# Softmax attentions of a two-block transformer: values at rest in TensorE, outputs turned back by head pairs, query tiles from last to first

## The reference, cut to what matters

```
def mla_attention(q_nope, q_rope, k_nope, k_rope, v):
    ...
        s = einsum('bqhd,bkhd->bhqk', qn, k_nope) + einsum('bqhd,bkd->bhqk', qr, k_rope)
        causal = key_pos[None, :] <= qpos[:, None]
        p = softmax(where(causal, s * scale, neg), axis=-1)
        return einsum('bhqk,bkhd->bqhd', p, v)

def dsa_attention(q, k, v, q_idx, k_idx, w_idx, topk):    # one key and value head for 4 query heads
    ...
        p = softmax(where(valid, einsum('bqhd,bhqj->bhqj', qb, k_sel) * scale, neg), axis=-1)
        return einsum('bhqj,bqjd->bqhd', p, v_sel)

def native_sparse_attention(...):                          # 2 key and value heads, 3 query heads each
    ...
        o_s = einsum('bgrqn,bgqnd->bqgrd', masked_softmax(s_s, key_pos <= tq), v_sel)
        o_w = einsum('bgrqn,bngd->bqgrd', masked_softmax(s_w, m_w), vw)
        return gt[:, :, 0] * o_c + gt[:, :, 1] * o_s + gt[:, :, 2] * o_w
```

## Time and profile before

| what | value |
|---|---|
| time of three runs, median | 3297.77 us (3294.56 to 4249.05) |
| time of the profiled execution | 3300.15 us |
| its span, first to last instruction | 3298.4 us |
| mean granted TensorE clock, share of full | 0.984 |
| PE busy | 3144.2 us, 95% |
| PE weight loads (PEld, beside PE) | 2651.6 us, 80% |
| VectorE (DVE) busy | 1812.1 us, 55% |
| ScalarE (ACT) busy | 1302.5 us, 39% |
| GpSimd (POOL) busy | 391.2 us, 12% |

### The profile page before, as it was taken

The page is one execution under the profiler, slowest core; times in us unless marked ns, Lnnn a source line. Parts: engine busy times, 40 slices in busy tenths (PEclk is TensorE's granted clock), DMA queues, the critical chain, the costliest instruction groups (busy, mean ns, idle before and its releaser), DMA issues. The chain is left out here.

```text
span 3298.4 us, 48870 instructions
## 1 busy us (share of the span) xinstructions
PE 3144.2 (95%) x19216; PEld 2651.6 (80%) x19216; DVE 1812.1 (55%) x3220; ACT 1302.5 (39%) x2692; POOL 391.2 (12%) x374
## 2 busy tenths in 40 slices
PE   8999999999999999979999999999899999999996
PEld 6878788877878888868888878888788878788885
DVE  4875443425865424337566457474475565574744
ACT  4454432334354413233374333233443653332324
POOL 1031000001040000001213302010004034010100
PEclk9999999999999999989999999999999999999998
DMA  4111222212202222132100122222222000222230
GB/s 169 55 52 39 90 91 101 90 69 91 74 1 77 90 99 93 51 105 104 65 1 2 40 83 99 91 101 87 73 99 85 1 2 28 83 93 93 93 110 35
DMA packets 37342, 239.55 MB, mean 73 GB/s; under 512 B 4464, under 2 KB 5232, under 8 KB 15088
## 3 DMA queue, kind: packets, MB, share of 16 engines
q1 hardware_dynamic: 36528, 234.21, 20.1%
q10 hardware_dynamic: 576, 2.10, 0.2%
HBM read 234.19 MB, written 2.10 MB: 72 GB/s over the span
## 5 line engine op out<-in xcount | busy, mean ns | idle before, releaser
L265 PE MATMUL ps<-b_hl,bff_whl 128*128 128x512 f32 x704 | 274.1, 389 | 3.1 <-DVE b_hl L667 3.1
L267 PE MATMUL ps<-b_hl,bff_whl 128*128 128x512 f32 x704 | 273.9, 389 | 0.0
L266 PE MATMUL ps<-b_hl,bff_whl 128*128 128x512 f32 x704 | 273.9, 389 | 0.0
L248 DVE SCALAR_TENSOR_TENSOR bff_whl<-ring,b_cols,bff_whl 128x512 fp32r<-128x512 f32 (+1 forms) x224 | 153.2, 745 | 197.3 <-ACT bff_whl L235 197.1
L245 DVE TENSOR_TENSOR aff_whl<-ring,aff_whl 128x512 fp32r<-128x512 f32 x160 | 99.8, 685 | 222.8 <-ACT aff_whl L233 222.7
L235 ACT ACTIVATE bff_whl<-ring,b_cols 128x512 fp32r<-128x512 f32 (+1 forms) x224 | 136.6, 682 | 176.4 <-PE ps L267 176.4
L266 PE MATMUL ps<-aff_whl,a_u 128*128 128x512 f32 x512 | 204.3, 399 | 0.0
L265 PE MATMUL ps<-a_hl,aff_whl 128*128 128x512 f32 x512 | 199.5, 390 | 3.1 <-DVE a_hl L667 3.1
L265 PE MATMUL ps<-aff_whl,a_u 128*128 128x512 f32 x512 | 201.7, 394 | 0.0
L267 PE MATMUL ps<-aff_whl,a_u 128*128 128x512 f32 x512 | 200.7, 392 | 0.0
L267 PE MATMUL ps<-a_hl,aff_whl 128*128 128x512 f32 x512 | 199.2, 389 | 0.0
(11 more groups left out here) (524 smaller groups left out, 7746.5 us busy)
## 6 DMA issues: line engine op xcount, KB each, us to landing
ring<-in_a_w_ff SPq DMA_DIRECT2D x64, 1024.0 KB, 4.6
ring<-in_b_w_up SPq DMA_DIRECT2D x32, 1024.0 KB, 4.7
ring<-in_a_w_in SPq DMA_DIRECT2D x16, 1024.0 KB, 5.9
ring<-in_b_w_down SPq DMA_DIRECT2D x16, 1024.0 KB, 4.6
ring<-in_b_w_in_att SPq DMA_DIRECT2D x12, 1024.0 KB, 4.7
ring<-in_b_w_up SPq DMA_DIRECT2D x16, 768.0 KB, 4.0
ring<-in_b_w_in_conv SPq DMA_DIRECT2D x12, 768.0 KB, 4.2
ring<-in_a_w_out SPq DMA_DIRECT2D x8, 1024.0 KB, 4.8
```

Of the source, the lines that this page charges most:

```text
L248: self.c.nc.vector.scalar_tensor_tensor(out=self.part(j, 1, k), in0=src[:, k, :], scalar=g[:, row + k:row + k + 1], in1=self.part(j, 0, k) ...
L265: nc.tensor.matmul(bank, sh, mh, start=start, stop=False)
L266: nc.tensor.matmul(bank, sh, ml, start=False, stop=False)
L267: return nc.tensor.matmul(bank, sl, mh, start=False, stop=stop)
```

## The change

A pair of heads is now the unit of output, and three things change in `softmax_attention`:
- The query tiles of a head run from last (t = 3, 512 keys) to first (128 keys). ScalarE copies the turned probabilities into a pT that keeps all four query tiles of a head, for two heads; the widest tile of each head is copied by VectorE (semaphore lastT).
- The value product has the values at rest: at unit (h, j) key tile j meets all query tiles from j on, since those have run: one product with (4 - j) x 128 moving columns, into bank 6. The tile at rest is 128 columns wide: 64 values of the head and 64 zeros, on the left for the first head of a pair and on the right for the second, so that both heads sum into one bank, the first in rows 0 to 63, the second in rows 64 to 127. The four tiles of both heads are one sum of eight products.
- After a pair VectorE copies bank 6 to oT (semaphore lifted), PE turns oT back with four transposes into bank 7 (returned), and VectorE multiplies from there by reciprocal sums and gates for both heads at once. Bank 6 is the only one of its kind: the first value product of the next pair waits on lifted.

In mla the causal mask is added by a product as in the others, with two tiles rounded by ScalarE in the stage ahead. `place` is GpSimd's new first job in each stage: zero fills beside the values (one of 4 x 4 x 64 columns in mla, two of 4 x 64 in dsa), in nsa two copies and two fills of 4 x 64. The nsa heads are paired across the key heads (0 with 3, 1 with 4, 2 with 5), and so is the order in which their queries are split.

```diff
+    def __init__(self, scores, values, mask, out, gate=None):
+        self.scores, self.values, self.mask, self.out, self.gate = scores, values, mask, out, gate
+def softmax_attention(c, name, pairs, place, meanwhile=None, beside=None, ready=None):
...
-    units = [(h, t) for h in range(len(heads)) for t in range(TT)]
-    U = len(units)
+    units = [(h, t) for h in range(2 * len(pairs)) for t in reversed(range(TT))]
+    U, last = len(units), TT - 1
+    by_act = lambda u: sum(t < last for _, t in units[:u + 1])
+    begins = lambda u: 0 <= u < U and units[u][1] == last
+    ends_pair = lambda u: 0 <= u < U and units[u][0] % 2 == 1 and units[u][1] == 0
...
+        p, pT = sb("p", [P, 3, SEQ]), sb("pT", [P, 2, TT, SEQ])
+        negmax, rsum, weight = sb("negmax", [P, 8]), sb("rsum", [P, 2, TT, 2]), sb("weight", [P, TT, 2])
+        oT, tmp = sb("oT", [P, SEQ]), sb("o", [P, TT, 2, HD])
+        wide = weight[:].unsqueeze(3).broadcast_to([P, TT, 2, HD])
+        turned_of = lambda u: c.ps[:, 4 + u % 2, 0:(units[u][1] + 1) * P].rearrange("p (j q) -> p j q", q=P)
+        kept_of = lambda u: pT[:, units[u][0] % 2, 0:units[u][1] + 1, units[u][1] * P:(units[u][1] + 1) * P]
...
+            @block.gpsimd
+            def _(pool):
+                step = Steps(pool, pool_step)
+                place(step).then_inc(placed, 1)
+                if meanwhile is not None:
+                    meanwhile(pool, step)
             @block.tensor
             def _(pe):
-                for i in range(U + 4):
+                for i in range(U + 6):
                     if i < U:
                         h, t = units[i]
                         nk = (t + 1) * P
                         if i >= 4:
                             pe.wait_ge(probs, i - 3)
-                        if t == 0 and ready is not None:
+                        if t == last and ready is not None:
                             ready(pe, beside_done, h)
...
+                        ident, mask = pairs[h // 2].mask(t)
+                        for n, (q, k) in enumerate(pairs[h // 2].scores(h % 2, t)):
+                            nc.tensor.matmul(c.ps[:, i % 4, 0:nk], q, k, start=(n == 0), stop=False)
+                        nc.tensor.matmul(c.ps[:, i % 4, nk - mask.shape[1]:nk], ident, mask,
+                                         start=False, stop=True).then_inc(scores, 1)
                     u = i - 2
                     if 0 <= u < U:
                         pe.wait_ge(probs, u + 1)
-                        if u >= 2:
-                            pe.wait_ge(probsT, u - 1)
+                        if begins(u - 2):
+                            pe.wait_ge(lastT, units[u - 2][0] + 1)
+                        elif u >= 2:
+                            pe.wait_ge(probsT, by_act(u - 2))
                         for j in range(units[u][1] + 1):
                             ins = nc.tensor.transpose(c.ps[:, 4 + u % 2, j * P:(j + 1) * P],
                                                       p[:, u % 3, j * P:(j + 1) * P], c.ident)
                         ins.then_inc(turned, 1)
                     u = i - 4
                     if 0 <= u < U:
...
+                        h, j = units[u]
+                        if j < last:
+                            pe.wait_ge(probsT, by_act(u))
+                        else:
+                            pe.wait_ge(lastT, h + 1)
+                            if h == 0:
+                                pe.wait_ge(placed, 1)
+                            elif h % 2 == 0:
+                                pe.wait_ge(lifted, h // 2)
+                        ins = nc.tensor.matmul(c.ps[:, 6, j * P:], pairs[h // 2].values(h % 2, j),
+                                               pT[:, h % 2, j, j * P:], start=(h % 2 == 0 and j == last),
+                                               stop=(h % 2 == 1 and j == 0), skip_group_check=True)
+                        if j == 0:
+                            ins.then_inc(outs, 1)
+                    u = i - 6
+                    if ends_pair(u):
+                        n = units[u][0] // 2
+                        pe.wait_ge(lifted, n + 1)
+                        if n:
+                            pe.wait_ge(kept, n)
+                        for t in range(TT):
+                            ins = nc.tensor.transpose(c.ps[:, 7, t * P:(t + 1) * P], oT[:, t * P:(t + 1) * P], c.ident)
+                        ins.then_inc(returned, 1)
                 c.stay_busy(pe, 0, 8)
             @block.vector
             def _(dve):
                 step = Steps(dve, step_sem)
-                for i in range(U + 5):
+                for i in range(U + 7):
                     if i < U:
-                        h, t = units[i]
-                        nk, mask = (t + 1) * P, heads[h].masks(t)
+                        nk = (units[i][1] + 1) * P
                         dve.wait_ge(scores, i + 1)
...
                         nc.vector.tensor_reduce(negmax[:, i % 8:i % 8 + 1], c.ps[:, i % 4, 0:nk],
                                                 AX.X, ALU.max, negate=True).then_inc(maxed, 1)
                         if beside is not None:
                             beside(dve, beside_done, i)
+                    u = i - 2
+                    if begins(u):
+                        h = units[u][0]
+                        dve.wait_ge(turned, u + 1)
+                        if h >= 2:
+                            dve.wait_ge(outs, h - 1)
+                        nc.vector.tensor_copy(kept_of(u), turned_of(u)).then_inc(lastT, 1)
                     u = i - 5
...
+                    if ends_pair(u):
+                        n = units[u][0] // 2
+                        dve.wait_ge(outs, 2 * n + 2)
+                        if n:
+                            dve.wait_ge(returned, n)
+                        nc.vector.tensor_copy(oT[:], c.banks(6)).then_inc(lifted, 1)
+                    u = i - 6
+                    if ends_pair(u):
+                        n = units[u][0] // 2
+                        pair = pairs[n]
+                        o = c.banks(7).rearrange("p (t b d) -> p t b d", t=TT, b=2)
+                        dve.wait_ge(probs, u + 1)
+                        step(nc.vector.reciprocal(weight[:], rsum[:, n % 2]))
+                        if pair.gate is not None:
+                            step(nc.vector.tensor_tensor(weight[:], weight[:], pair.gate, ALU.mult))
+                        dve.wait_ge(returned, n + 1)
+                        if pair.gate is None:
+                            nc.vector.tensor_tensor(pair.out, o, wide, ALU.mult).then_inc(kept, 1)
                         else:
...
+                            step(nc.vector.tensor_tensor(tmp[:], o, wide, ALU.mult))
+                            nc.vector.tensor_tensor(pair.out, pair.out, tmp[:], ALU.add).then_inc(kept, 1)
             @block.scalar
             def _(act):
-                for i in range(U + 3):
+                for i in range(U + 2):
                     if i < U:
                         h, t = units[i]
                         nk = (t + 1) * P
                         act.wait_ge(maxed, i + 1)
                         if i >= 3:
                             act.wait_ge(turned, i - 2)
-                        if t == 0 and h >= 4:
-                            act.wait_ge(kept, h - 3)
+                        if t == last and h % 2 == 0 and h >= 4:
+                            act.wait_ge(kept, h // 2 - 1)
                         nc.scalar.activation(p[:, i % 3, 0:nk], c.ps[:, i % 4, 0:nk], ACT.Exp,
                                              bias=negmax[:, i % 8:i % 8 + 1],
-                                             accum_out=rsum[:, h % 4, t:t + 1]).then_inc(probs, 1)
+                                             accum_out=rsum[:, h // 2 % 2, t, h % 2:h % 2 + 1]).then_inc(probs, 1)
                     u = i - 2
-                    if 0 <= u < U:
-                        nk = (units[u][1] + 1) * P
+                    if 0 <= u < U and not begins(u):
+                        h, t = units[u]
                         act.wait_ge(turned, u + 1)
...
+                        if t == last - 1 and h >= 2:
+                            act.wait_ge(outs, h - 1)
+                        nc.scalar.copy(kept_of(u), turned_of(u)).then_inc(probsT, 1)
...
-                transpose_tiles(c, "mlaT", jobs)
+                def rounded(act):
+                    nc.scalar.copy(ident_m[:], c.ident)
+                    nc.scalar.copy(causal_m[:], c.causal)
+                transpose_tiles(c, "mlaT", jobs, None, rounded)
+                def zeros_beside_values(step):
+                    return nc.gpsimd.memset(kv4[:, :, 1::2, 0:MLA_NOPE], 0.0)
...
+                two = lambda a: a.rearrange("p t (b d) -> p t b d", b=2)
                 softmax_attention(c, "mla", [
...
+                    AttentionPair(lambda b, t, n=n: [(qT[0:MLA_QK, 2 * n + b, t * P:(t + 1) * P],
```

(45 more changed lines are left out.)

82 lines of the change are left out of this document (16 added, 66 removed).

## The result

The changed kernel takes 3345.59 us (median of three runs, 3342.49 to 3347.08) where the kernel before takes 3297.77: ratio 1.0148, 95% interval 1.0119 to 1.0178. One run of the kernel before came out slow, at 4249.05, and the ratio is taken without it. The change costs 48 us; I forecast 63. The interval leaves no doubt that it is slower, but by the limit of about 2% that is still no change, and it lies in the range.

The account below looks back on a forecast made before the run. PE was taken to bound the attention stages. Value products +20.3, turning +11.0, mask +4.5 and -1.9, new wait +27.9 and +4.3, fills and ends -1, small waits -2 gave +63.1: 3361 us, range 3328 to 3385.

Parts of the forecast that it names:

- The new wait: PE at pair starts waits for VectorE's copy of bank 6: 18 times 1.55 us, +27.9, plus 4.3 for side jobs.
- rival 4: Stalls at pairs lower the granted clock, 1.7 us lost at each of 24 pairs: +41, 3402 us; chance 0.07.
- Rival 1: The wait for the copy of bank 6 is mostly absorbed: 3333 us; chance 0.13.
- Value products: On PE, eight wide records replace twenty narrow ones a head, priced by their columns like f32 scores: +20.3 us.
- Rival 2: Wide value product records on PE are cheap, nearly as cheap as narrow ones: 3286 us; chance 0.04.
- Mask product: In mla, 64 mask products on PE at 0.07 us: +4.5; a wait gone with VectorE's add: -1.9.
- Turning back: Four PE transposes per pair of heads, 0.46 us for each of 24 pairs: +11.0 us.
- Small nsa waits: Small waits of PE in the nsa stages partly go: -2 us.
- rival 3: At transposes of nsa's 512-key unit, VectorE or ScalarE comes 0.4 us late in 24 heads: +10, 3371; chance 0.14.
- fills and ends: Filling the pipeline with the widest unit first and ending stages with the narrow one: -1 us in all six stages.
- The signs that I had named: Expected in the profile after: wide records 0.43 us apart, mla head 6.4 us, nsa head about 5.6, waits for VectorE's copy.
- The sign for "too fast": PE waiting for ScalarE at transposes in each head, or granted clock below 0.95 inside stages, would show the forecast too fast.

Follow-up runs that it names:

- narrow run: The changed kernel with each value product cut to 128 query columns, 768 of 1280 columns a head left out: 3296.72 us, ratio to before 0.9997.
- copy first: The changed kernel with VectorE's copy of bank 6 put ahead of the maximum of the same step: 3316.32 us, ratio to before 1.0059.
- two banks: The changed kernel with pairs summed in banks 6 and 7 by turns and turned back into the same bank: 3318.55 us, ratio to before 1.0068.
- both copies first: The changed kernel with VectorE's copy of bank 6 ahead of the maximum and ScalarE's copy ahead of its exponential: 3309.68 us, ratio to before 1.0036.
- the copy of ScalarE alone: The changed kernel with only ScalarE's copy of the turned probabilities ahead of the present unit's exponential: 3338.12 us, ratio to before 1.0121.
- the kernel with 64-column products: The changed kernel with each value product cut to 64 query columns, the rest left out: 3305.00 us, ratio to before 1.0019.

## Why the prediction was right or wrong

The direction, the verdict and the main cause were right; the size was 15 us too large.

*The new wait: right in mechanism and place, and nearer in size than it deserved.* I had 18 x 1.55 + 4.3 = 32.2 us. There are 18 waits, 1.41 late in a plain one; the one behind nsa's side job is 1.97 idle. Taking them away gives 27 and 29 us, but some 5 of these are lower clock (rival 4). That leaves 22 to 24 for the waits themselves, 8 to 10 under my sum: the chain was 0.14 shorter each time, and a little of the standing still was taken up elsewhere. Rival 1 (mostly absorbed) is out.

*Value products: this term was mis-sized, and made up most of the miss.* I priced them at 2.39 us a head by the f32 scores of before, "which have the same widths and two passes". In mla they measured 2.17: the score rows held 0.05 of open weight load each, since a score product before stood behind a 64-column value product whose columns are shorter than a load. And the same 0.05 leaves the scores now that wide products stand ahead of them, which I hadn't counted. So an mla head pays 0.17 for the products and gets 4 x 0.05 = 0.20 back from the scores. In nsa the two together went from 3.75 to 3.69. If a dsa head is like an nsa head, the term is some -2 us where I had 20.3.

*Rival 2* would have had wide products nearly free. The narrow run shows that they aren't: 768 columns fewer a head are worth 49 us. The Trainium skill's 131 ns for a product of 512 columns (TensorE: Matmul & The Clock Gate, section Back-to-back issue gap) doesn't hold for this kernel's f32 products, whose starts are 0.43 us a pass apart. That the term came out near nothing has another reason, the load that the wide products cover.

*Mask product:* 4.5 less 1.9 forecast; alone it measured 2 by a steady head and nothing by its time, since it also took away 3.0 us of mla's waits for ScalarE's copy. Too large by 2 to 3 us, within the noise of the runs.

*Turning back:* 24 x 0.43 = 10.3, 11.0 forecast; leaving out three quarters of it bore the rows out. Right. The rows, timeline of PE after, mla:

```profile
236.19 0.60 PE L2412 MATMUL ps<-const_a,mlaoT 128*128 128x128 f32 x4
...
236.62 0.60 PE L2375 MATMUL ps<-a_kT,a_qT 96*128 96x256 f32 x2
```

*Small nsa waits:* forecast to go (-2); they grew. In nsa ScalarE's copy held the transposes before in 6 places, 6 x 0.44 = 2.6; after in 14, 14 x 0.42 = 5.9. That is rival 3 in its place and size, which I had computed with the exponential alone. I missed the second semaphore of the same instruction, the copy that stands behind that exponential. Removing it gives 7.5 us, more than these 5.9: 1.1 of the rest are the dsa stages, what is left is not placed. The waits that did go are mla's, 3.8 us in 8 places, which I hadn't looked for.

*Rival 4:* partly true, and I gave it 0.07. The granted clock did fall inside attention, for instance right behind the longest nsa wait. Windows of the kernel after, ahead of that stretch and in it, and in the like stretch of the second mla stage:

```profile
1674.00:1684.00 10.00, 7.78 (x47) 5.89 (x46) 5.96 (x11) 5.52 (x20) 0.00 (x0) 1.00 0.01 2
1684.60:1688.00 3.40, 3.40 (x16) 3.02 (x15) 2.45 (x6) 0.83 (x3) 0.00 (x0) 0.53 0.00 0
937.20:940.70 3.50, 3.50 (x13) 2.69 (x11) 1.07 (x3) 0.83 (x3) 3.42 (x3) 0.51 0.00 0
```

It is the level of 1.2 GHz. It happened at three of 18 pair starts, not at 24: in the second mla stage and in both nsa stages, each time just after a wait of 1.86 or 1.97 us, the longest of its stage. Each cost 1.7 us (3.5 us at 0.51), the price that I had put on it, so 5.1 us. No such stretch is there in the profiled runs of the kernel before and of the three that have no wait for bank 6 (copy first, two banks, both copies first); in these the clock in the attention stages is 1.00 but for the start of nsa, which is low in all kernels. The narrow run, which keeps the waits, has one, and the copy of ScalarE alone has three. So the fall goes with the wait, and its 5 us are part of the 29 that the copy first gives. The mean granted clock of the whole run, 0.984 before and after, hides it, because other stages vary by as much.

*The signs that I had named.* The passes of the wide value products do start 0.43 us apart. The steady mla head takes 5.70 us, 5.9 with its share of a turning, where I had 6.4. The sign for "too fast", a clock below 0.95 inside a stage, was there in nsa (0.93, of which the stage's start is a part).

*Sum.* By medians, the kernel with both copies first takes away 35.9 of the 48 us: the wait for bank 6, the clock that falls behind it, and the waits for ScalarE's copy. The turning is 10.3 of the 12.1 that stay. Some 2 us are left for the mask, the wide products, and the fills and ends together, and no run splits them. My -1 for fills and ends was too hopeful: the ends grew by 4, of which the six last turnings are 2.6. So the forecast came within 15 us with one term 20 too large, and with small waits, ends and clock too small: the sum is better than its parts. No run tested the order of the query tiles by itself.

## What to carry to other kernels

Price a tensor product by the longer of its moving columns and the load of the weights behind it, and price its neighbours anew when its width changes: a row of the trace already holds what its old neighbour left open. When an accumulator becomes the only one of its kind, its evacuation belongs ahead of other work in that engine's order, or the accumulator needs a second bank; here that one line was worth 29 of 48 us, some 5 of them by a clock that no longer fell. For each waiting instruction, run the sum for every semaphore it waits on, not for the one that seems latest.

## What the runs showed of the hardware that I had not expected

- A 128x128 weight load and 128 moving f32 columns of one pass both take about 0.11 us: value products of 64 and of 128 columns give the same head, 4.59 us, to the hundredth.
- A wait of less than 2 us can bring a loss of clock nearly as large as itself: in three of 18 places the granted clock fell to 1.2 GHz right behind the longest waits, for 3.5 us, which costs 1.7. There is one profiled run of each kernel; in those without the waits it did not happen.
- Less work on PE can go with less clock: the kernel with 64-column products showed a granted clock of 0.90 in an nsa stage where the one with 128 columns had 0.97, and took 8 us more; its runs at the usual clock did not. That the one causes the other is not shown.
- The same swap on ScalarE, copy before exponential, gave 7 us in one order of units and cost 3 in the other.
